# Recurrence gates of a hybrid decoder layer: each 64-wide head on its own 64 rows of the array, both gates side by side in its columns

## The reference, cut to what matters

```
xh = xf.reshape(bsz, s, 16, 64)                       # xf: the convolved branch
r = sigmoid(einsum('bshi,hij->bshj', xh, w_r) + b_r)  # recurrence gate
i = sigmoid(einsum('bshi,hij->bshj', xh, w_i) + b_i)  # input gate
log_a = -8.0 * r * softplus(-lam)
u = sqrt(-expm1(2.0 * log_a)) * (i * xf)
h_t = exp(log_a_t) * h_{t-1} + u_t                    # scan over the tokens
```

## Time and profile before

| | |
|---|---|
| median of three runs | 887.32 us (887.18 to 887.77) |
| span of the profiled execution, first to last instruction | 884.2 us |
| outside the span (median less span) | 3.1 us |
| mean granted clock of TensorE | 0.984 |
| PE busy | 837.3 us, 95% |
| DVE busy | 342.1 us, 39% |
| ACT busy | 272.0 us, 31% |
| HBM read | 246.89 MB |

### The profile page before, as it was taken

The page is one execution under the profiler, slowest core; times in us unless marked ns, Lnnn a source line. Parts: engine busy times, 40 slices in busy tenths (PEclk is TensorE's granted clock), DMA queues, the critical chain, the costliest instruction groups (busy, mean ns, idle before and its releaser), DMA issues.

```text
span 884.2 us, 10342 instructions
## 1 busy us (share of the span) xinstructions
PE 837.3 (95%) x4281; PEld 528.8 (60%) x4281; DVE 342.1 (39%) x478; ACT 272.0 (31%) x397; POOL 82.0 (9%) x61
## 2 busy tenths in 40 slices
PE   4999999999999999899999999988898898999996
PEld 4888888787888888436535354352352352533685
DVE  6899549962652616511020120101100101015865
ACT  7666347733332236202010100101001001002777
POOL 3436370000000000000000000000000000001000
PEclk9999999999999999999999999999899999999998
DMA  9222222211525764999999999999999999998902
GB/s 261 95 94 96 95 96 96 96 49 50 188 96 210 293 258 180 357 422 421 398 429 427 429 425 427 427 428 428 427 428 428 427 425 431 427 421 347 356 2 95
DMA packets 45334, 253.85 MB, mean 287 GB/s; under 512 B 8868, under 2 KB 9960, under 8 KB 31976
## 3 DMA queue, kind: packets, MB, share of 16 engines
q1 hardware_dynamic: 42696, 248.21, 69.2%
q0 software_dynamic: 2304, 4.20, 1.2%
q10 hardware_dynamic: 288, 0.79, 0.2%
HBM read 246.89 MB, written 10.49 MB: 291 GB/s over the span
## 4 chain that ended last, share of the span: by engine, by line
PE 73%; DMA 16%; DVE 4%; ACT 2%; SPq 2%; issue 2%; DVEq 0%; ACTq 0%
PE bank L1434 72%; DMA ring<-in_w_down_e_dram 15%; PE bank L1647 1%; DVE ring L1121 1%; DVE ring L1101 1%; DMA ring<-in_w_in_dram 1%; ACT ring_rounded L405 1%; SPq L522 1%; DMA ring<-in_w_up_b_dram 1%; SPq L517 0%; PE bank L1740 0%; PE bank L1499 0%; ACT L1024 0%; ACT ring L778 0%; DVE pick L1228 0%
## 5 line engine op out<-in xcount | busy, mean ns | idle before, releaser
L1434 PE MATMUL bank<-ring_rounded,ring_rounded 128*128 128x512 f32 (+1 forms) x696 | 244.7, 389 | 0.1
L1434 PE MATMUL bank<-r_rounded,ring_rounded 128*128 128x512 f32 (+1 forms) x744 | 234.4, 389 | 0.8 <-DVE ring_rounded L1059 0.8
L1434 PEld LDWEIGHTS bank<-r_rounded,ring_rounded 128*128 128x128 f32 x744 | 138.9, 188 | 30.7 <-DVE ring_rounded L1059 1.0
L1434 PEld LDWEIGHTS bank<-ring_rounded,ring_rounded 128*128 128x128 f32 x696 | 130.5, 188 | 27.5 <-issue 0.7
L1434 PE MATMUL bank<-ring,gain 128*64 128x512 f32 x472 | 118.0, 603 | 8.3 <-issue 8.2
L1434 PE MATMUL bank<-ring,hT 128*64 128x512 f32 x400 | 113.7, 627 | 6.5 <-DMA ring<-in_w_down_e_dram 6.5
L1434 PE MATMUL bank<-ring,junk 128*64 128x512 f32 x472 | 115.4, 592 | 0.0
L1434 PEld LDWEIGHTS bank<-ring,gain 128*64 128x64 f32 x472 | 35.9, 138 | 75.4 <-issue 72.4
L1434 PEld LDWEIGHTS bank<-ring,junk 128*64 128x64 f32 x472 | 37.4, 137 | 71.6 <-issue 71.5
L717 POOL DMA_INDIRECT expert_rows<-r,row_i x16 | 16.6, 1035 | 669.4 <-DVE r L1321 669.4
L923 ACT ACTIVATE r<-bank,factor 128x512 f32<-128x512 f32 x16 | 11.0, 688 | 216.6 <-PE bank L1434 216.6
(11 more groups left out here) (217 smaller groups left out, 760.6 us busy)
## 6 DMA issues: line engine op xcount, KB each, us to landing
ring<-in_w_up_e_dram SPq DMA_DIRECT2D x29, 2048.0 KB, 29.4
ring<-in_w_gate_e_dram SPq DMA_DIRECT2D x24, 2048.0 KB, 28.0
ring<-in_w_down_e_dram SPq DMA_DIRECT2D x22, 2048.0 KB, 32.3
ring<-in_w_in_dram SPq DMA_DIRECT2D x18, 1024.0 KB, 7.3
r<-in_w_gate_e_dram SPq DMA_DIRECT2D x5, 2048.0 KB, 27.5
r<-in_w_down_e_dram SPq DMA_DIRECT2D x4, 2048.0 KB, 34.4
ring<-in_w_down_e_dram SPq DMA_DIRECT2D x7, 1024.0 KB, 21.7
ring<-in_w_up_e_dram SPq DMA_DIRECT2D x6, 1024.0 KB, 10.6
```

The lines of the kernel that those rows point to most:

```text
L1434: return nc.tensor.matmul(*a, **k)
```

## The change

- `diag` becomes `heads`: one 128 x 128 matrix for each c. Head 2c has rows 0-63 and head 2c+1 rows 64-127. In the columns the two gates' matrices stand side by side: recurrence, input for the even head, and input, recurrence for the odd one. Nothing is zero any more, so the zeroing on POOL and SP's wait for it go.
- A product takes 64 rows of `heads` and 64 rows of the convolved tile and gives 128 columns: both gates of one head. For each c there are still six, in three pairs; the two of a pair use different rows and different banks.
- In a bank the two gates of one head now share the partitions in halves, so each sigmoid becomes two, of 64 partitions each; two of the four read one half of the partitions and write the other.
- The input gate's bias is loaded with its halves swapped, in two loads in place of one.
- The two splits of the gate matrices are half as large.

```diff
-        diag = r3[:, 0:NX * 2 * P].rearrange("p (c w j) -> p c w j", c=NX, w=2)
+        heads = r3[:, 0:NX * P].rearrange("p (c j) -> p c j", c=NX)
...
-                          b_rg[0].rearrange("(c p) -> c p", p=P), b_ig[0].rearrange("(c p) -> c p", p=P),
+                          b_rg[0].rearrange("(c p) -> c p", p=P), None, ...
+                    if v is None:
+                        swapped = b_ig[0].rearrange("(c two p) -> c two p", two=2, p=HD)
+                        for odd in range(2):
+                            sp.dma_start(vecs[row:row + NX, HD * (1 - odd):HD * (2 - odd)], swapped[:, odd, :]).then_inc(small_in, 16)
...
-                sp.wait_ge(zero_ready, 1)
                 for w, src in enumerate((w_rg, w_ig)):
                     for odd in range(2):
-                        sp.dma_start(diag[64 * odd:64 * odd + 64, :, w, 64 * odd:64 * odd + 64],
+                        at = HD * (w ^ odd)
+                        sp.dma_start(heads[HD * odd:HD * odd + HD, :, at:at + HD],
...
-            nc.gpsimd.memset(diag[:, :, :, :], 0.0).then_inc(zero_ready, 1)
...
-            nc.scalar.activation(diag_high, diag, ACT.Copy).then_inc(diag_high_ready, 1)
+            nc.scalar.activation(heads_high, heads, ACT.Copy).then_inc(heads_high_ready, 1)
...
-                after(nc.scalar.activation(lru_t[:, b, :], bank[4 + 2 * b][:, :], ACT.Sigmoid, bias=col(5, c)))
-                nc.scalar.activation(lru_i[:, b, :], bank[5 + 2 * b][:, :], ACT.Sigmoid, bias=col(6, c)).then_inc(i_ready, 1)
+                even, odd = slice(0, HD), slice(HD, P)
+                nc.scalar.activation(lru_t[even, b, :], bank[4 + 2 * b][even, :], ACT.Sigmoid, bias=col(5, c)[even, :])
+                after(nc.scalar.activation(lru_t[odd, b, :], bank[5 + 2 * b][odd, :], ACT.Sigmoid, bias=col(5, c)[odd, :]))
+                nc.scalar.activation(lru_i[even, b, :], bank[4 + 2 * b][odd, :], ACT.Sigmoid, bias=col(6, c)[odd, :])
+                nc.scalar.activation(lru_i[odd, b, :], bank[5 + 2 * b][even, :], ACT.Sigmoid,
+                                     bias=col(6, c)[even, :]).then_inc(i_ready, 1)
...
-            v.tensor_tensor(diag_low, diag, diag_high, ALU.subtract).then_inc(diag_low_ready, 1)
+            v.tensor_tensor(heads_low, heads, heads_high, ALU.subtract).then_inc(heads_low_ready, 1)
...
-            pe.wait_ge(small_in, 16 * 6)
+            pe.wait_ge(small_in, 16 * 7)
...
-                for w in range(2):
-                    dst = bank[4 + 2 * (c % 2) + w][:, :]
-                    mm(dst, diag_high[:, c, w, :], xc_high(c), start=True, stop=False)
-                    mm(dst, diag_low[:, c, w, :], xc_high(c), start=False, stop=False)
-                    ins = mm(dst, diag_high[:, c, w, :], xc_low(c), start=False, stop=True)
+                for n, (w, x_) in enumerate(((heads_high, xc_high), (heads_low, xc_high), (heads_high, xc_low))):
+                    for odd in range(2):
+                        rows = slice(HD * odd, HD * odd + HD)
+                        ins = mm(bank[4 + 2 * (c % 2) + odd][:, :], w[rows, c, :], x_(c)[rows, :], start=(n == 0), stop=(n == 2))
```

More of the change, by code:

```diff
@@ L53, in build @@
     HALF = D // 2
+    HD = w_rg.shape[2]
     FAR = 4096
@@ L58, in build @@
     TEAMS = NE // TEAM
-    assert NE % 4 == 0 and S == 512 and D == 1024
+    assert NE % 4 == 0 and S == 512 and D == 1024 and 2 * HD == P
     loads = [(which, e) for which in range(2) for e in range(2)]
@@ L124, in h1T @@
             return (r4[:, 0:D], gain[:, :])[i % 2].rearrange("p (k t) -> p k t", k=KD)
-        diag = r3[:, 0:NX * 2 * P].rearrange("p (c w j) -> p c w j", c=NX, w=2)
-        wpool = r3[:, NX * 2 * P:NX * 2 * P + NB * P].rearrange("p (g j) -> p g j", g=NB)
+        heads = r3[:, 0:NX * P].rearrange("p (c j) -> p c j", c=NX)
+        wpool = r3[:, NX * P:NX * P + NB * P].rearrange("p (g j) -> p g j", g=NB)
         scr = ring[:, 5:7, :].rearrange("p s w -> p (s w)")
@@ L136, in build @@
         gel = scr[:, 10 * S:12 * S].rearrange("p (b t) -> p b t", b=2)
-        diag_high = slot_r[7][:, 0:NX * 2 * P].rearrange("p (c w j) -> p c w j", c=NX, w=2)
-        diag_low = r3_r[:, 0:NX * 2 * P].rearrange("p (c w j) -> p c w j", c=NX, w=2)
+        heads_high = slot_r[7][:, 0:NX * P].rearrange("p (c j) -> p c j", c=NX)
+        heads_low = r3_r[:, 0:NX * P].rearrange("p (c j) -> p c j", c=NX)
         def xc_high(c):
@@ L148, in build @@
         xbp = r4[:, :].rearrange("p (g t) -> p g t", g=NB)
-        o = NX * 2 * P + NB * P
+        o = NX * P + NB * P
         wsum = r3[:, o:o + 2 * W].rearrange("p (b t) -> p b t", b=2)
@@ L274, in build @@
         pool_step = sem("pool_step")
-        zero_ready = sem("zero_ready")
         vec_psum = sem("vec_psum")
@@ L294, in build @@
         conv_done = sem("conv_done")
-        diag_high_ready = sem("diag_high_ready")
-        diag_low_ready = sem("diag_low_ready")
+        heads_high_ready = sem("heads_high_ready")
+        heads_low_ready = sem("heads_low_ready")
         xc_high_ready = sem("xc_high_ready")
@@ L514, in small_loads @@
                 for v in (conv_w[0].rearrange("w (c p) -> (w c) p", p=P), conv_b[0].rearrange("(c p) -> c p", p=P),
-                          b_rg[0].rearrange("(c p) -> c p", p=P), b_ig[0].rearrange("(c p) -> c p", p=P),
-                          lru_lambda[0].rearrange("(c p) -> c p", p=P), pool_scale[0].rearrange("(c p) -> c p", p=P)):
+                          b_rg[0].rearrange("(c p) -> c p", p=P), None, lru_lambda[0].rearrange("(c p) -> c p", p=P), pool_scale[0].rearrange("(c p) -> c p", p=P)):
+                    if v is None:
+                        swapped = b_ig[0].rearrange("(c two p) -> c two p", two=2, p=HD)
+                        for odd in range(2):
+                            sp.dma_start(vecs[row:row + NX, HD * (1 - odd):HD * (2 - odd)], swapped[:, odd, :]).then_inc(small_in, 16)
+                        row += NX
+                        continue
                     sp.dma_start(vecs[row:row + v.shape[0], :], v).then_inc(small_in, 16)
                     row += v.shape[0]
-                sp.wait_ge(zero_ready, 1)
                 for w, src in enumerate((w_rg, w_ig)):
                     for odd in range(2):
-                        sp.dma_start(diag[64 * odd:64 * odd + 64, :, w, 64 * odd:64 * odd + 64],
+                        at = HD * (w ^ odd)
+                        sp.dma_start(heads[HD * odd:HD * odd + HD, :, at:at + HD],
                                      src[0].rearrange("(c two) i j -> two i c j", two=2)[odd]).then_inc(lru_in, 16)
@@ L1092, in _ @@
             v.reciprocal(rcount[:, :], rcount[:, :]).then_inc(prm_ready, 1)
-            dve.wait_ge(diag_high_ready, 1)
-            v.tensor_tensor(diag_low, diag, diag_high, ALU.subtract).then_inc(diag_low_ready, 1)
+            dve.wait_ge(heads_high_ready, 1)
+            v.tensor_tensor(heads_low, heads, heads_high, ALU.subtract).then_inc(heads_low_ready, 1)
             def conv(c):
@@ L1469, in lru_gates @@
                 if c == 0:
-                    pe.wait_ge(diag_low_ready, 1)
-                for w in range(2):
-                    dst = bank[4 + 2 * (c % 2) + w][:, :]
-                    mm(dst, diag_high[:, c, w, :], xc_high(c), start=True, stop=False)
-                    mm(dst, diag_low[:, c, w, :], xc_high(c), start=False, stop=False)
-                    ins = mm(dst, diag_high[:, c, w, :], xc_low(c), start=False, stop=True)
+                    pe.wait_ge(heads_low_ready, 1)
+                for n, (w, x_) in enumerate(((heads_high, xc_high), (heads_low, xc_high), (heads_high, xc_low))):
+                    for odd in range(2):
+                        rows = slice(HD * odd, HD * odd + HD)
+                        ins = mm(bank[4 + 2 * (c % 2) + odd][:, :], w[rows, c, :], x_(c)[rows, :], start=(n == 0), stop=(n == 2))
                 ins.then_inc(gates_psum, 1)
```

## The result

| | before | after |
|---|---|---|
| median of 20 runs each | 886.94 us | 888.14 us |
| after / before, 95% interval | | 1.0016 (1.0009 to 1.0024) |
| span of the profiled execution | 884.2 us | 886.1 us |
| granted clock of TensorE | 0.984 | 0.984 |
| gate 3 starts on PE | 56.21 us | 57.98 us |

The ratio is +1.4 us, between 0.8 and 2.1. The median was forecast to 0.4 us (888.5). A profile is a single execution: the runs of the kernel before take 1.7 to 1.8 us more than their own span, not 3.1, so its profiled one was about 1 us quicker than its median; the one after was 0.2 quicker.

What follows compares the result with a forecast made beforehand. SP, ACT and DVE were taken to bound the kernel until gate 3, PE after it. 1.04 + 1.7 - 1.58 gave +1.2 us on the 884.2 us span, so a median of 888.5 us, range 886.3 to 890.4.

Steps and rivals of the forecast that it cites:

- What bounds the kernel: SP, ACT and DVE up to 56.21 us, then PE alone; PE's shift at the front's end is the kernel's.
- The sigmoids: On ACT, four of 64 partitions at full price each, 0.58 us apart: each gate's tanh comes 1.16 us later.
- SP's issue: One more vector load ahead of the weights at 20.05 us, costing 0.33 us in full on the path.
- The pairs: Gate products on PE: two 64-row products run in the time of one, three pairs taking 0.68 us a gate.
- the rival of turns: Row halves on PE run one after the other: a gate takes 1.59 us, time 890.0 us; chance 0.22.
- The passages: PE's going into and out of the 64-row form costs 0.23 us a gate, so a gate saves 0.45.
- dear passages: PE runs empty at each change of form: a gate takes 1.46 us, time 889.3 us; chance 0.09.
- The stand: PE waits 3.05 us before gate 3, which starts at 57.70 us, losing what gates 0 to 2 save.
- The clock: After PE's wait before gate 3, the granted clock likely falls to half for 3.4 us, costing 1.7 us.
- The second four: Gates 4 to 7 on PE save 1.58 us net, with a wait of 0.22 us before gate 7.
- The clock stays up: No fall of the granted clock after PE's wait before gate 3: -0.5 us, 886.8 us; chance 0.27.
- Half-height sigmoids at half price: Each sigmoid of 64 partitions on ACT costs half: -1.9 us, time 885.4 us; chance 0.06.

Runs made afterwards that it cites:

- Experiment 1: Kernel before with each sigmoid in two halves of 64 partitions, products, loads and splits unchanged: median 888.83 us, ratio 1.0022 (1.0010 to 1.0034).
- experiment 3: Changed kernel with 11 products nobody reads put ahead of gate 3: median 887.20 us, ratio 1.0005 (0.9994 to 1.0016) against the kernel before.

## Why the prediction was right, and where a term was off

- **What bounds the kernel.** Right. PE took over at gate 3, and the shift of PE at the front's end, +1.87 us, is that of the end: the span grew by 1.9. From the first expert to the end it is 521.0 to 522.0 us in all fourteen profiles, so nothing is given back there. That both kernels took 33.37 us from the router to the first expert was luck: with falls and fills nine of the other twelve took 0.4 to 2.7 more. The view of waits has one more wait of PE's weight loads for DVE behind the first 20 us, which the earlier trace rows leaves out: 0.8 us in the router, before and after.
- **The sigmoids** were mis-sized: I took 2 x 0.58 = 1.16 us for two more, and they cost 2.82 - 1.31 = 1.51. The 0.58 was read between two whole activations of which neither waits for the other; half-height ones come 0.70 to 0.71 apart with or without a wait. Why they do not follow as closely as whole ones is not shown. The Trainium skill (ScalarE: Activation LUTs, the section on ACT_TABLE_LOAD) gives 280 ns and 0.833 ns a column for tiles of 128 partitions, an estimate of 0.71 us for 512 columns; the trace has 0.69 for 128 partitions and for 64.
- **SP's issue** was 0.24 us at ACT in place of 0.33; with the sigmoids gate 3 came at +1.77 in place of +1.49. Experiment 1 gives the sigmoids' part by itself. That of the issue is 0.12 us in the mean of nine profiles, and half of the 0.24 cannot be told from scatter. The splits, costed at nothing, did hide: ACT's wait for the weights only grew, from 1.01 to 1.77 us.
- **The pairs** were right (0.24 us, two in the time of one), and the rival of turns fell. The estimate of 0.30 from the Trainium skill (TensorE: Matmul & The Clock Gate, part 3), made from four row tiles, was too dear for these two halves of the rows.
- **The passages** were mis-sized: 0.39 us for the two, where I took 0.23. A gate saves 0.25, not 0.45; "dear passages" was half true.
- **The stand** was forecast at 3.05 us by starts, and PE could have begun at 54.37 + 4 x 0.227 = 55.28 us, so it was 2.70: later low half, but slower PE. In it the entry to the form was hidden, and gate 3 of the kernel before, which stood too, had taken 1.51 us (56.21 to 57.72) and not 1.36. So gate 3 came out 0.51 shorter: +1.26 behind it, against +1.04 in the sum.
- **The clock** was right in kind and size: 3.4 us at 0.50, and PE's shift goes from +1.26 to +2.89; experiment 3 takes it away.
- **The second four** save 0.97 us in place of 1.58 (from +2.89 to +1.92), each gate 0.25. Gate 7 waits for nothing of note: tanh 4 held DVE up by 0.74 us, and DVE's low half ended at 151.00, PE came at 151.03.
- **The rivals.** "The clock stays up" needed that stand to be harmless; 1.56 us in experiment 1 was, 2.54 was not. Length alone does not decide it: in the earlier trace rows 2.17 us was followed by a fall and 2.86 was not. Half-height sigmoids at half price are refuted by the first row of the sigmoids.

Against the sum of +1.2 us that is 0.22 more behind gate 3, 0.07 less for the clock and 0.61 more in the last four: +1.9, as profiled. The interval of the ratio, 0.8 to 2.1 us, holds both. That the medians, too, differ by 1.2 is luck in part: the terms as measured do not add up to it.

## What to carry to other kernels

Before a product is made cheaper, see whether its engine waits right behind it: here three gates' savings went into a stand, and the clock fell behind the stand. Splitting an activation by partitions doubled its price here, so a layout that halves the rows on TensorE is paid on ScalarE; put what is needed late behind what is needed first, and most of the split hides. When a transfer is brought forward, look at whom it sets free, and what that then collides with.

## What the runs showed that I had not expected

- One operation of DVE on 128 x 8 took 4.57 us in place of 0.17, because POOL had begun a low half of 4.60 us just before it.
- Going from whole-array products to pairs of row halves and back costs 0.39 us together, in four steps of 0.09 to 0.11: before and behind the first product of either form.
- Half-height activations start 0.70 us apart even where nothing makes them wait; whole ones were 0.58 apart there.
- Stands of 2.54, 2.75 and 3.80 us in the front were each followed by a granted clock of 0.50 for 3.4 us, those of 0.86 to 1.56 us by none; in the router a fall came in twelve of fourteen profiles, at different places in kernels that do the same there, and cost nothing where a stand behind it took it up.
